# Gates of a PEER layer loaded for eight keys at a time, and the last norm's factors loaded late into buffers that have come free

## The reference

```python
ALPHA = (2.0 * DEPTH) ** 0.25
for l in range(DEPTH):
    ...
    x = layer_norm(ALPHA * x + mix, ln1_g[l], ln1_b[l])
    ffn = peer_ffn(x, w_query[l], sub_keys[l], expert_u[l], expert_v[l])
    x = layer_norm(ALPHA * x + ffn, ln2_g[l], ln2_b[l])

def block(xb):                      # peer_ffn, for 128 tokens
    ...                             # product keys give idx, 8 heads x 16 experts, and their scores
    g = jax.nn.softmax(best_s, axis=-1)
    u = expert_u[idx]
    h = jax.nn.gelu(jnp.einsum('thkd,td->thk', u, xb), approximate=False)
    w = (g * h).astype(xb.dtype)
    return jnp.einsum('thk,thkd->td', w, expert_v[idx])
```

## Time and profile before

| | before |
|---|---|
| time, median of 3 runs | 2881.89 us |
| the profiled execution, its own time | 2883.32 us |
| its span (first to last instruction) | 2881.2 us |
| TensorE busy | 2615.7 us (91%) |
| VectorE busy | 2259.3 us (78%) |
| ScalarE busy | 921.4 us (32%) |
| GpSimd busy | 1284.1 us (45%) |
| expert phase | from 1165 to 2881 us |

### The profile page before, as it was taken

How to read it: one execution, slowest core, us unless ns; L and a number is a source line. 1 busy time by engine, 2 the same in 40 slices (tenths; PEclk the granted TensorE clock), 3 DMA queues, 4 the chain that set the end, 5 groups by cost and what they waited for, 6 DMA issues and landing times.

```text
span 2881.2 us, 47367 instructions
## 1 busy us (share of the span) xinstructions
PE 2615.7 (91%) x17256; PEld 1716.3 (60%) x17459; DVE 2259.3 (78%) x4541; ACT 921.4 (32%) x1603; POOL 1284.1 (45%) x869
## 2 busy tenths in 40 slices
PE   7999888989867755899999999999999999999996
PEld 3566655659867754565565565565565665665652
DVE  3244454646999998688888988898788998988997
ACT  2333233531125545422232232232232232332324
POOL 2110020110024441366665666676456666666762
PEclk9999997999979975899999999999999999999998
DMA  4000202440002243899999999999799999999995
GB/s 159 23 16 16 81 1 65 144 150 2 1 8 125 120 189 150 322 381 355 349 360 355 347 345 366 347 342 368 264 359 355 353 362 359 340 362 361 347 327 197
DMA packets 274015, 682.23 MB, mean 237 GB/s; under 512 B 29448, under 2 KB 111880, under 8 KB 269456
## 3 DMA queue, kind: packets, MB, share of 16 engines
q0 software_dynamic: 110592, 402.70, 37.6%
q1 hardware_dynamic: 163216, 276.73, 27.0%
HBM read 622.73 MB, written 56.62 MB: 236 GB/s over the span
## 4 chain that ended last, share of the span: by engine, by line
PE 55%; DVE 8%; issue 8%; POOL 4%; DMA 2%; ACT 1%; POOLq 0%; DVEq 0%; SPq 0%; ACTq 0%
PE h_psum L1939 28%; PE o_psum L1950 26%; POOL rt_hot L1263 3%; DVE rt_top_u L1311 1%; DMA early<-u_blocks 1%; DVE rt_top L1309 1%; DVE rt_hot L1454 1%; DVE rt_hot L1444 1%; DVE rt_scores L1313 1%; DVE rt_pos L1329 1%; PE r_t_psum L1099 1%; DVE rt_best L1327 0%; POOL rt_cand L1247 0%; DVE wide L1793 0%; DVE rt_found L1395 0%
## 5 line engine op out<-in xcount | busy, mean ns | idle before, releaser
L1939 PE MATMUL h_psum<-early 128*128 128x384 bf16 (+1 forms) x6144 | 863.2, 301 | 14.9 <-DVE early L1759 13.9
L1950 PE MATMUL o_psum<-v_split,w_split 128*128 128x512 bf16 x3681 | 823.7, 380 | 18.2 <-DVE v_split L1766 8.7
L1939 PEld LDWEIGHTS h_psum<-early 128*128 128x128 bf16 x6144 | 603.8, 98 | 273.9 <-issue 21.5
L1950 PEld LDWEIGHTS o_psum<-v_split,w_split 128*128 128x128 bf16 x3840 | 376.3, 98 | 445.5 <-DVE v_split L1766 9.1
L1728 POOL DMA_INDIRECT early<-u_rows,pick_index x320 | 446.3, 1395 | 302.6 <-DVE dots L1789 178.2
L1728 POOL DMA_INDIRECT early<-v_blocks,pick_index x320 | 446.5, 1395 | 246.1 <-DVE wide L1793 170.5
L1793 DVE SCALAR_TENSOR_TENSOR wide<-early,dots,wide 128x1024 f32<-128x1024 f32 x320 | 404.2, 1279 | 15.6 <-DMA early<-v_blocks,pick_index 14.9
L1789 DVE CUSTOM_DVE_ANT_0 early<-early,wide 128x1024 f32<-128x1024 f32 x320 | 385.4, 1217 | 11.3 <-DMA early<-u_rows,pick_index 10.9
L1649 ACT ACTIVATE act_out<-h_psum 128x384 f32<-128x384 f32 (+1 forms) x256 | 97.9, 434 | 614.2 <-PE h_psum L1939 614.2
L1657 ACT ACTIVATE v_split<-early 128x512 bf16<-128x512 f32 x256 | 159.8, 625 | 346.7 <-PE o_psum L1950 341.2
L1099 PE MATMUL r_t_psum<-x_t,early 128*128 128x128 f32 (+1 forms) x1920 | 232.9, 282 | 0.0
(11 more groups left out here) (211 smaller groups left out, 2944.1 us busy)
## 6 DMA issues: line engine op xcount, KB each, us to landing
early<-u_blocks SPq DMA_DIRECT2D x128, 512.0 KB, 7.3
early<-v_blocks SPq DMA_DIRECT2D x256, 256.0 KB, 6.1
gates<-wide SPq DMA_DIRECT2D x20, 2048.0 KB, 6.4
gate<-gates SPq DMA_DIRECT2D x32, 1280.0 KB, 20.0
early<-w_query SPq DMA_DIRECT2D x8, 1024.0 KB, 5.9
early<-w_fox SPq DMA_DIRECT2D x4, 1536.0 KB, 6.9
early<-u_rows,pick_index POOLq DMA_INDIRECT x320, 7.9
early<-v_blocks,pick_index POOLq DMA_INDIRECT x320, 7.5
```

The source lines that it names most:

```text
L1939: mm = pe.matmul(h_psum[:, half, 0:width * P], u_split[:, q % 2, part, c], xs[:, first:first + width, xpart, c, :], start=(c == 0 and part ...
L1950: mm = pe.matmul(o_psum[t][:, :], w_split[:, w_slot(r, q), part, t * P:(t + 1) * P], v_split[:, k, vpart], start=(q == 0 and part + vpart ...
```

## The change

A gate buffer holds eight keys (`GATE_KEYS`) instead of four, so a run in HBM is 1 KB instead of 512 bytes. A group is loaded in two parts of ten chunks, 1280 KB each, so there are still 32 loads of that size. At the phase's start both parts of group 0 are issued; group 1 follows inside the first `refill`, at its steps 1 and 3. In later periods the parts of a buffer are issued when all its eight keys have been multiplied: after 8 and 12 blocks for the first group of the next period, after 16 blocks and after 4 blocks of the next period for the second. VectorE waits for both parts at each eighth block. The tiles for `ln_g` and `ln_b` are gone; their values are loaded into the two raw U slots in the last period, behind its sixteenth V refill, once the last U block is split.

```diff
+GATE_KEYS = SPAN // 2
...
-        gate = sb("gate", [P, 2, TOKENS // CHUNK, GROUP, CHUNK], F32)
+        gate = sb("gate", [P, 2, TOKENS // CHUNK, GATE_KEYS, CHUNK], F32)
...
-        ln_g = sb("ln2_g_sb", [P, D_MODEL], F32)
-        ln_b = sb("ln2_b_sb", [P, D_MODEL], F32)
+        ln_g, ln_b = u_raw[:, 0], u_raw[:, 1]
...
-                def load_gate(i, g):
-                    sp.dma_start(gate[:, g % 2], gates[:, :, bass.ds(SPAN * i + g * GROUP, GROUP), :]
+                def load_gate(i, g, part):
+                    some = slice(part * TOKENS // CHUNK // 2, (part + 1) * TOKENS // CHUNK // 2)
+                    sp.dma_start(gate[:, g % 2, some], gates[:, some, bass.ds(SPAN * i + g * GATE_KEYS, GATE_KEYS), :]
                                  ).then_inc(gate_in[g % 2], 16)
...
-                        done = q + AHEAD
-                        if done % GROUP == 0 and not (end and done // GROUP + 2 > SPAN // GROUP):
+                        done, part = q + AHEAD, (q + AHEAD) % GATE_KEYS // 4
+                        if first and done in (AHEAD + 1, AHEAD + 3):
+                            load_gate(0, 1, done // 2 - 1)
+                        if done % 4 == 0 and done >= GATE_KEYS and not end:
                             sp.wait_ge(gated, SPAN * i + done)
-                            load_gate(i, done // GROUP + 1)
+                            load_gate(i, done // GATE_KEYS + 1, part)
+                        if done == 4 and not first:
+                            sp.wait_ge(gated, SPAN * i + done)
+                            load_gate(i, 1, 1)
...
-                        if first and q == 2 * DENSE + 1:
-                            sp.dma_start(ln_g[:, :], ln2_g.partition_broadcast(P)).then_inc(ln_in, 16)
-                        if first and q == 2 * DENSE + 3:
-                            sp.dma_start(ln_b[:, :], ln2_b.partition_broadcast(P)).then_inc(ln_in, 16)
+                        if end and q == SPAN - 1:
+                            sp.wait_ge(u_lo_done, N_KEYS)
+                            sp.dma_start(ln_g, ln2_g.partition_broadcast(P)).then_inc(ln_in, 16)
+                            sp.dma_start(ln_b, ln2_b.partition_broadcast(P)).then_inc(ln_in, 16)
...
-                load_gate(0, 0)
+                load_gate(0, 0, 0)
+                load_gate(0, 0, 1)
...
-                load_gate(0, 1)
...
-                    g, q = b // GROUP, b % GROUP
+                    g, q = b // GATE_KEYS, b % GATE_KEYS
                     dve.wait_ge(gelu_done, b + 1)
                     if q == 0:
-                        dve.wait_ge(gate_in[g % 2], 16 * (g // 2 + 1))
+                        dve.wait_ge(gate_in[g % 2], 32 * (g // 2 + 1))
```

More of the change, by code:

```diff
@@ L1867, in scale_rows @@
                     dve.wait_ge(mean_made, t + 1)
-                    dve.scalar_tensor_tensor(acc[:, t], acc[:, t], neg_mean[:, t:t + 1], ln_g[:, :], ALU.add, ALU.mult
+                    dve.scalar_tensor_tensor(acc[:, t], acc[:, t], neg_mean[:, t:t + 1], ln_g, ALU.add, ALU.mult
                                              ).then_inc(scaled, 1)
@@ L1887, in finish @@
                     dve.wait_ge(rstd_step, 5 * t + 5)
-                    dve.scalar_tensor_tensor(acc[:, t], acc[:, t], rstd[:, t:t + 1], ln_b[:, :], ALU.mult, ALU.add
+                    dve.scalar_tensor_tensor(acc[:, t], acc[:, t], rstd[:, t:t + 1], ln_b, ALU.mult, ALU.add
                                              ).then_inc(rows_done, 1)
```

## The result

The changed kernel takes 2888.78 us (median of 10 runs, 2885.99 to 2890.87), the kernel before beside it 2881.72 us (median of 10, 2878.34 to 2884.63). The ratio is 1.0023 with a 95% interval of 1.0014 to 1.0033, which is 4.0 to 9.5 us slower. The predicted time was 2886.4 us with a range of 2882.0 to 2889.8 us: the time lies within it, but beyond the 5.8 us up to which the likeliest case called it no change. It lies where rival A put it (2888.5 us).

The account below looks back on a forecast made before the run. TensorE bounds the middle, so only the ends count: start +3.0, clock +0.2, between the ends 0, tail +1.3 give +4.5 us on 2881.9, 2886.4 us; range 2882.0 to 2889.8 us.

Parts of the forecast that it names:

- the likeliest case: Whole kernel: measured time within 5.8 us of the kernel before, not told from no change; chance 0.67.
- rival A: Tail, 2805 to 2826: norm's loads hit the gathers in full, 2.6 us, slower broadcast up to 2 more; 2888.5 us, chance 0.26.
- What bounds the kernel: Middle of expert phase: TensorE busy 248.7 of 250 us; a lighter gate load gives nothing there, only the ends count.
- the 0 us between the ends: Between start and tail: gate waits, strides and U refills cost nothing, 0 us, at most 1 us either side.
- Start, +3.0 us: Phase start: two gate parts, 7.5 us for 4.5, delay the third U block TensorE waits for; bounds +1.9 and +4.5.
- the line between two packet rows: Gate loads: 9 ns per packet plus 0.037 ns per byte, so 1 KB runs go at 348 GB/s, 3.8 us per part.
- SP's issues: SP's queue: packet number unchanged at the start, issues held no more than before; later U refills held up to 8.3 us, less after.
- The clock, +0.2 us: Phase start: TensorE's idle time grows from 4.0 to 7.0 us, half clock costs 0.2 us more, between 0 and 0.9.
- Tail, +1.3 us: Last takes: late norm factors' 1.05 MB compete with gathers; half of 2.6 us taken, bounds 0 and 2.6.
- The hole of 1.18 MB: Tail, 2806 to 2814: engines move only 264 GB/s, leaving 1.18 MB of room for the factors' loads, not fully usable.
- The sum: Whole kernel: 3.0 + 0.2 + 0 + 1.3 = +4.5 us, forecast 2886.4 us, 0.16% more; chance 0.50.
- rival C: Tail: lighter gates relieve the gathers, VectorE's 3.7 us of waits go, 2881.4 us; chance 0.06.

Follow-up runs that it names:

- both old loads at the start: Kernel before, with only the second gate load (keys 4 to 7, 512-byte runs) issued right behind the first, ahead of the third U block; ratio 1.0018.

## Why the prediction was right, and where not

**What bounds the kernel** was read rightly. TensorE's stream from the fourth `up` to the last half period takes 1598 us before and after, and what was lost lies at the two ends. ScalarE's shorter waits for U blocks (68.3 to 12.5 us) bought nothing, as the 0 us between the ends said.

**Start, +3.0 us.** Measured +3.2 us in the first profiles and 2.9 in the mean of two each (17.8 and 18.0 against 14.6 and 15.1). The step was the rate of 1 KB runs on the line between two packet rows, 348 GB/s. The packets of the stretch 1184 to 1188, nearly all of them 1 KB after, and nearly all of them 512 bytes in the kernel with both old loads at the start:

```profile
DMA packets 1395, 1.43 MB, mean 357 GB/s; under 512 B 17, under 2 KB 1393, under 8 KB 1394
```
```profile
DMA packets 2296, 1.17 MB, mean 292 GB/s; under 512 B 16, under 2 KB 2296, under 8 KB 2296
```

That is 357 GB/s, and 292 GB/s where the prediction had worked out 290 from a mixed stretch; the 4.6 us that one more old load cost there say the same. This term was right in its mechanism and its size.

**SP's issues.** That they would be held back no more than before was wrong in its place, not in its effect: the third U load was issued at 1178.32, 3.65 us behind the first gate load, where it had been 0.7. But it stands in the queue behind the gates' bytes either way. For the U refills behind later gate loads the prediction read too little from its row: before, SP was held for up to 10.64 us at one (at 2102.03), not 8.3; after, for at most 1.4.

**The clock, +0.2 us.** There is next to nothing of it. The third `up` took 9.2 and 9.4 us in the two profiles after, 9.2 and 9.2 in those before. In the twelve profiles with the U blocks behind the gates it took 8.0 to 9.4 us after idle times of 7.2 to 10.0 us and 8.4 to 9.4 us after 4.0 to 5.8 us, so the longer idle time made the clock no worse.

**Tail, +1.3 us.** This term was mis-sized, and the step that failed is its price: the factors' loads were priced by their bytes alone (1.05 MB, 2.6 us, of which half was taken). The hole of 1.18 MB was there, and in the one profile that tried it, it took 1.05 MB of ordinary loads at no cost that can be seen. The broadcast, however, costs 2.5 to 3.2 us, more than all its bytes at full rate (2.6 us) at the upper end. The prediction had the row for it: 14.4 and 9.1 us to landing against 7.3 us of a U block. But only rival A used it, and the sum left it out. It was a weak row, as U blocks of before land after anything from 3.4 to 22.6 us. On the Trainium skill's rule to issue early and wait late ("DMA: Bandwidth & Descriptors", "Rules for kernel authors"): the factors were waited for nowhere, so by it the place was safe; the runs show that the late loads delay others (2.5 to 3.2 us), which the rule does not speak of.

**The sum.** That the measured time lies inside the stated range is partly luck: the range was drawn wide enough for rival A, while in the sum half the bytes' price (+1.3 us) stood for a cost that is not one of bytes. That the first profile of the changed kernel showed just these 1.3 us was luck too; its repeat shows 1.7 to 2.7 us against the two profiles of before. With the measured terms the sum is 2.9 to 3.2 at the start and 2.5 to 3.2 at the tail, 5.4 to 6.4 us, within the interval of 4.0 to 9.5 us; the 0.9 us by which the phase may begin later would come on top. A small relief goes the other way: without late factors the tail is 38.0 us in the new gate order and 38.8 in the old one, with them 40.5 and 42.0. So rival C is not quite empty, but the 0.8 to 1.5 us rest on a few profiles, and it stays open how the gates would matter there, as the last gate load is issued 78 us before the restart in the kernel before (2722.7) and 116 us before it after (2689.5). The likeliest outcome, no change that can be told (within 5.8 us), did not come true; the median is 7.1 us up. Rival A comes nearest, by its second half, the slower broadcast, and it had a chance of 0.26; its first half, that the hole takes too few bytes, is not what the runs show.

## What to carry to other kernels

A larger load that relieves the steady state can still cost time at the one place where no other work covers it: look at what stands behind the first issue in the queue, and whether the first consumer needs all of it. Ask also which of two loads the bounding engine waits for first, and issue that one first; here that was worth 6 us with neither load changed. When a load is moved, price not only its bytes but its form, and against whom it runs.

## What the runs showed of the hardware

- One row of 4 KB broadcast to 128 partitions beside random gathers: the second of two landed after 7.5 to 8.6 us (five profiles), an ordinary load of the same size in the same place after at most 5.7 (one profile), and the engines moved 350 to 365 in the place of 379 GB/s in the 20 us around it.
- Stretches in which nearly all packets had one size: 512 bytes 292 GB/s (both old loads at the start), 1 KB 357 GB/s (after), over 2 KB 411 GB/s (before).
- Of two gate loads issued back to back, the second kept SP longer with shorter runs of the same number of bytes: both issues together took 9.06 us with 512-byte runs (both old loads at the start) and 3.60 us with 1 KB runs (after).
- Two profiles of the same kernel differ by up to 1.4 us in the tail (after: 39.7 and 41.1) and by up to 1.0 us in where the phase begins (before: 1167.06 and 1168.01). A difference of 1 us needs more than one of each.
